# A decoder step on one core: output tiles begun inside the last pair, and the decode step's first half in sixteen pieces there

## The reference, cut to what matters

```python
# layer 0, per token t and head: state S of 64 x 64 (decode: one step on the loaded state)
sa = einsum('bhij,bhj->bhi', S, -kk_t)
S  = S * w_t[:, :, None, :] + sa[..., None] * (kk_t * a_t)[:, :, None, :] + v_t[..., None] * k_t[:, :, None, :]
y  = einsum('bhij,bhj->bhi', S, r_t)
...
out = y_gated @ w_out                       # (512 + 8) x 1024 by 1024 x 1024
...
kv  = h @ kv_w_a                            # 1024 x (256 + 64)
c_kv, k_pe = rmsnorm(kv[..., :256]), rope(kv[..., None, 256:], pos)[:, :, 0]
q   = einsum('btr,rhe->bthe', rmsnorm(q_a), w_q)   # 384 -> 8 heads x (128 + 64)
q_nope, q_pe = q[..., :128], rope(q[..., 128:], pos)
```

## Time and profile before

| | |
|---|---|
| median of three runs | 1195.48 us (1194.74 to 1195.77) |
| the profiled execution | 1196.15 us |
| its span, first to last instruction | 1194.3 us |
| mean granted TensorE clock | 0.954 |
| TensorE matmuls busy | 1074.7 us (90%) |
| VectorE busy | 512.7 us (43%) |
| ScalarE, GpSimd busy | 301.0 us, 105.7 us |

### The profile page before, as it was taken

The page is one execution under the profiler, slowest core; times in us unless marked ns, Lnnn a source line. Parts: engine busy times, 40 slices in busy tenths (PEclk is TensorE's granted clock), DMA queues, the critical chain, the costliest instruction groups (busy, mean ns, idle before and its releaser), DMA issues.

```text
span 1194.3 us, 26039 instructions
## 1 busy us (share of the span) xinstructions
PE 1074.7 (90%) x11683; PEld 767.1 (64%) x11683; DVE 512.7 (43%) x922; ACT 301.0 (25%) x565; POOL 105.7 (9%) x138
## 2 busy tenths in 40 slices
PE   2698999999999999998668887999999999999993
PEld 0466777777777767676533565887683766665563
DVE  0594455454646464555549535101120445442104
ACT  2113222223232232223011122132202344443101
POOL 0002000111111010101014120000000001000100
PEclk9799999999999999999889888999999899999897
DMA  8501021221203040402335344211211123332001
GB/s 341 210 1 71 3 89 58 75 74 59 89 10 138 2 145 2 146 2 78 139 105 223 142 195 157 88 53 64 82 71 54 71 89 125 142 131 101 1 1 71
DMA packets 18015, 110.48 MB, mean 93 GB/s; under 512 B 6888, under 2 KB 9712, under 8 KB 11760
## 3 DMA queue, kind: packets, MB, share of 16 engines
q1 hardware_dynamic: 10640, 84.57, 18.9%
q0 software_dynamic: 2304, 20.97, 4.7%
q10 hardware_dynamic: 4960, 3.27, 0.9%
HBM read 103.35 MB, written 5.19 MB: 91 GB/s over the span
## 4 chain that ended last, share of the span: by engine, by line
PE 73%; DVE 11%; issue 5%; ACT 3%; DMA 0%; ACTq 0%; DVEq 0%
PE pj L945 19%; PE pj L1378 7%; PE bk L1055 7%; PE pj L1309 5%; PE pj L1435 3%; PE pj L1305 2%; PE bk L1407 2%; PE bk L1488 2%; PE bk L878 2%; PE bk L1472 2%; PE bk L1473 1%; PE bk L1317 1%; PE bk L1010 1%; PE pj L974 1%; PE pj L1501 1%
## 5 line engine op out<-in xcount | busy, mean ns | idle before, releaser
L945 PE MATMUL pj<-XM,ring 128*128 128x260 f32 x1024 | 261.4, 396 | 0.9 <-DVE XM L1729 0.9
L945 PEld LDWEIGHTS pj<-XM,ring 128*128 128x128 f32 x1024 | 183.5, 190 | 40.6 <-issue 12.1
L1378 PE MATMUL pj<-XM,ring 128*128 128x260 f32 x352 | 80.6, 393 | 0.0
L1378 PEld LDWEIGHTS pj<-XM,ring 128*128 128x128 f32 x352 | 68.8, 196 | 11.0
L1055 PEld LDWEIGHTS bk<-arena,ring 64*64 64x64 f32 x2560 | 45.9, 137 | 35.9 <-issue 29.3
L1055 PE MATMUL bk<-arena,ring 64*64 64x64 f32 x2560 | 56.9, 228 | 8.6 <-DVE arena L1816 5.1
L878 PE MATMUL bk<-ring,cT 128*9 128x512 f32 x240 | 35.1, 685 | 21.1 <-DMA ring<-in_ada 21.1
L1822 DVE TENSOR_TENSOR arena<-arena,bk 128x512 f32<-128x512 f32 x40 | 27.5, 688 | 61.5 <-PE bk L1055 61.5
L1954 DVE TENSOR_SCALAR arena<-bk 128x512 f32<-128x512 f32 x4 | 2.8, 692 | 105.2 <-PE bk L1331 73.7
L1816 DVE TENSOR_TENSOR arena<-bk,arena 128x512 f32<-128x512 f32 x40 | 27.7, 691 | 35.0 <-PE bk L1055 34.8
L2034 DVE TENSOR_TENSOR bk<-bk,arena 128x128 f32<-128x128 f32 x32 | 9.6, 299 | 72.2 <-PE bk L1473 37.0
(11 more groups left out here) (341 smaller groups left out, 1837.6 us busy)
## 6 DMA issues: line engine op xcount, KB each, us to landing
ring<-in_ada SPq DMA_DIRECT2D x16, 2048.0 KB, 8.6
ring<-in_w_in SPq DMA_DIRECT2D x8, 2048.0 KB, 7.4
ring<-in_b_w_in SPq DMA_DIRECT2D x3, 2048.0 KB, 16.7
R<-in_xT SPq DMA_DIRECT2D x2, 2080.0 KB, 14.2
ring<-in_w_out SPq DMA_DIRECT2D x2, 2048.0 KB, 8.0
ring<-in_w_q SPq DMA_DIRECT2D x2, 1536.0 KB, 6.2
out_y<-R SPq DMA_DIRECT2D x4, 520.0 KB, 2.7
XM<-in_Sd SPq DMA_DIRECT2D x1, 2048.0 KB, 17.9
```

Source lines behind the costliest of these rows:

```text
L945: last = mm(pj[:, s, a, 0:HALF], w[:, e, k, :], XM[:, e, k, a * HALF:(a + 1) * HALF], start=(k == 0), stop=(k == KT - 1))
L1378: last = mm(pj[:, t % 2, a, 0:HALF], w[:, k, e * P:(e + 1) * P], H1[:, k, a * HALF:(a + 1) * HALF], start=(k == 0), stop=(k == KT - 1))
```

## The change

The text below numbers its parts.

1. In the last pair TensorE does `early_part(u0, u1)`: units u = 0 to 31 are one 512-column matmul each of output tiles 0 to 3 (k = u // 4, tile u % 4), 28 of them between the steps of the pair (k = 0 to 6) and four after it. `late_ada(0)` leaves the pair. To have the weights, `stream` begins with `w_out`; the late modulation groups follow in another order.
2. The six decode factors are turned in the last pair, after `chunk_products`, and stored and moved by ScalarE ahead of `operands`; plain products wait for the store (`s_dta`).
3. The product and the reduction for `sa` run as 16 pieces of 8 rows each: two in each of the levels 1 to 4 between `level_z` and `level_t`, seven in the scan, one after `center`.
4. The product of 64 x 64 for `yd` and its reduction stay behind the loop; the two products that GpSimd had go to VectorE, behind the decode result.
5. Decode rows of all 8 output tiles go through `first_rows`, in four column groups at once, behind tile 7; tiles 4 to 7 have 512 columns (`first_tile`). `out_rows(1)` in the tail uses the four groups too.
6. Key/value tiles lose the 64 swapped columns (320 instead of 384); VectorE takes the halves crosswise.
7. The queries lose their four swapped tiles (12 instead of 16). ScalarE stores the four rotary tiles, SP swaps their halves by 8 DMAs, and VectorE combines them from there. The four `qz` DMAs move behind the decode queries' latents.

The order of the ring's loads and what frees a slot:

```diff
-        stream = [("ada", LATE), ("w_out", 0), ("w_out", 1), ("ada", LATE + 1), ("ada", LATE + 2), ("ada", LATE + 3),
-                  ("b_w_in", 0), ("b_w_in", 1), ("b_w_in", 2), ("kv_w_a", 0), ("w_q", 0), ("w_q", 1), ("uk", 0)]
+        stream = [("w_out", 0), ("w_out", 1), ("ada", LATE), ("ada", LATE + 2), ("ada", LATE + 3), ("ada", LATE + 1),
+                  ("b_w_in", 0), ("b_w_in", 1), ("b_w_in", 2), ("kv_w_a", 0), ("w_q", 0), ("w_qr", 0), ("uk", 0)]
...
-            return {"w_out": (s_om, KT) if g else (s_ow, 1), "kv_w_a": (s_kvm, 5), "b_w_in": (s_bm, QT + 4 * g),
-                    "w_q": (s_bm, B_K if g else B_PE), "uk": (s_bm, B_L + 1)}[name]
+            return {"w_out": (s_ow, g + 1), "kv_w_a": (s_kvm, 5), "b_w_in": (s_bm, QT + 4 * g),
+                    "w_q": (s_bm, B_PE), "w_qr": (s_bm, B_K), "uk": (s_bm, B_L + 1)}[name]
```

SP:

```diff
-            for n in range(3, len(stream)):
+            for n in (5, 3, 4, *range(6, len(stream))):
                 sp.wait_ge(*used(n - 3))
                 load(n)
-                if n == 3:
-                    sp.wait_ge(s_dd, 4)
+                if n == 4:
+                    sp.wait_ge(s_dd, 3)
                     sp.dma_start(o["wkv_s"], Sd).then_inc(s_dso, 16)
 
+            sp.wait_ge(s_ba, B_K)
+            for b in range(4):
+                dst, src = slice(b * 32, b * 32 + 32), slice((b ^ 1) * 32, (b ^ 1) * 32 + 32)
+                sp.dma_start(qa[dst], QP[src, 0:QT, :]).then_inc(s_qsw, 16)
+                sp.dma_start(rtmp[dst], QP[src, QT, :]).then_inc(s_qsw, 16)
```

TensorE:

```diff
+            def early_part(u0, u1):
+
+                n = SI[("w_out", 0)]
+                w = ring[:, n % 3, :].rearrange("p (k e) -> p k e", k=KT)
+                for u in range(u0, u1):
+                    k, t = u // SPL, u % SPL
+                    if u == 0:
+                        arrived(n)
+                        pe.wait_ge(s_ra, 7 * PAIRS)
+                        pe.wait_ge(s_ada_out, ADA_FIRST + PAIRS - 1)
+                    if t == 0:
+                        pe.wait_ge(s_yT, k + 1)
+                    last = mm(pj[:, t // 2, t % 2, :], w[:, k, t * P:(t + 1) * P], R1[:, k, 0:T],
+                              start=(k == 0), stop=(k == KT - 1))
+                    if k == KT - 1:
+                        last.then_inc(s_om, 1)
+
+            def turn_factors():
+                pe.wait_ge(s_pp, 3 * PAIRS)
...
                 chunk_products(m, 0)
                 if more:
                     project(m + 1, 0, 4, 6)
+                else:
+                    turn_factors()
+                    early_part(0, 2)
+                    pe.wait_ge(s_dta, 1)
                 plain_products(m)
                 value_products(m)
                 turn_a(m)
                 if more:
                     project(m + 1, 0, 6, KT)
+                else:
+                    early_part(2, 4)
                 for l in range(NLEV):
                     level_z(m, l)
...
-                    elif l in (1, 2):
-                        late_ada(0, l - 1, l)
+                    else:
+                        early_part(4 + 3 * l, 6 + 3 * l)
                     level_t(m, l)
...
+                    else:
+                        early_part(6 + 3 * l, 7 + 3 * l)
                 if more:
                     project(m + 1, 3, 6, KT)
+                else:
+                    early_part(19, 20)
                 inverse_products(m)
                 if more:
                     project(m + 1, 2, 0, 2)
+                else:
+                    early_part(20, 22)
                 transition_products(m)
                 chunk_inputs(m)
                 if more:
                     project(m + 1, 2, 2, 3)
+                else:
+                    early_part(22, 23)
                 for ch in range(1, NCH):
                     scan(m, ch)
...
+                    else:
+                        early_part(20 + ch, 21 + ch)
...
+            def first_rows(g):
+
+                w = out_weights(0, g)
+                for k in range(KT):
+                    j = k % 4
+                    last = mm(bk[j * G32:j * G32 + NS, 3 - g, :], R1[:, k, T:N], w[:, k, :], start=(k < 4), stop=(k >= 4))
+                last.then_inc(s_ow, 1)
...
+            early_part(28, 32)
+            first_tile(4)
+            ada(0)
+            first_tile(5)
             ada_turn(0)
...
+            first_tile(6)
+            ada(1)
+            first_tile(7)
+            ada_turn(1)
             pe.wait_ge(s_ydm, 32)
-            tr(pj[:, 1, 1, 0:HD], ydt[0:HD, :], ident[0:HD, 0:HD]).then_inc(s_ydt, 1)
-            ada(1)
+            tr(bk[:, 2, 0:HD], ydt[0:HD, :], ident[0:HD, 0:HD]).then_inc(s_ydt, 1)
             pe.wait_ge(s_r1, 1)
...
+            first_rows(0)
+            first_rows(1)
+            turn_first_rows()
             finish_sums(0)
             ada(2)
...
-            pe.wait_ge(s_ba, B_L + 1 - 8)
+            pe.wait_ge(s_ba, B_L + 1)
             pe.wait_ge(s_qpd, 64)
             scores(0)
```

VectorE (behind the loop, the product for `yd`, its reduction and the small sums stay as they were):

```diff
+            def decode_piece(n):
+
+                step, i0 = n // 8, n % 8 * 8
+                rows = slice(i0, i0 + 8)
+                if n == 0:
+                    dve.wait_ge(s_dq, 32)
+                    dve.wait_ge(s_sd, 16)
+                    then(V.tensor_tensor(wr, dq[:, 0, :], dq[:, 5, :], ALU.mult))
+                if step % 2 == 0:
+                    x = dq[:, 3, :] if step == 0 else wr
+                    then(V.tensor_tensor(Wd1[:, rows, :], Sd[:, rows, :], x.unsqueeze(1).to_broadcast([P, 8, HD]), ALU.mult))
+                else:
+                    mark(V.tensor_reduce((sa if step == 1 else yd)[:, rows], Wd1[:, rows, :], AX_X, ALU.add))
...
             then(V.tensor_tensor(r1d, r1d, decbuf[:, 7, :, :], ALU.mult), s_r1)
-            dve.wait_ge(s_dp, 1)
+            then(V.tensor_tensor(Wd2, bj(dq[:, 2, :]), bi(1), ALU.mult))
+            mark(V.tensor_tensor(Sd, Sd, bi(5), ALU.mult))
             then(V.tensor_tensor(Wd2, Wd2, Wd1, ALU.subtract))
-            dve.wait_ge(s_dp, 2)
             then(V.tensor_tensor(Sd, Sd, Wd2, ALU.add), s_dd)
...
+            dve.wait_ge(s_qsw, 128)
             for i in range(4):
...
+                x = qa[:, i, :] if i < QT else rtmp
+                mark(V.tensor_tensor(QP[:, i, :], QP[:, i, :], cosT, ALU.mult))
+                then(V.tensor_tensor(x, x, sinT, ALU.mult))
+                then(V.tensor_tensor(QP[:, i, :], QP[:, i, :], x, ALU.add), s_bd)
```

ScalarE, behind the loop and at the `qz` DMAs:

```diff
+            for t in range(5):
+                first_tile(t)
             ada_rows(0)
...
+            first_tile(5)
             ada_tiles(0)
...
+            act.wait_ge(s_dd, 1)
             then(A(rsd, bag[:, 1:2], ACT.Ln, bias=GN_EPS))
             mark(A(rsd, rsd, ACT.Exp, scale=-0.5), s_dr)
...
+            act.wait_ge(s_dd, 2)
             for hp in range(2):
                 act.dma_start(ydt[0:HD, hp * HD:(hp + 1) * HD], yd[hp * HD:(hp + 1) * HD]).then_inc(s_ydm, 16)
...
+            first_tile(6)
...
             act.wait_ge(s_bm, base + H + 2 * TT + 1)
+            act.wait_ge(s_bd, KT + 4)
+            act.wait_ge(s_zq, 1)
+            for hp in range(2):
+                for e in range(2):
+                    act.dma_start(qz[e * ROPE:(e + 1) * ROPE, e, hp:H:2, :], QP[hp * ROPE:(hp + 1) * ROPE, :, T:N]).then_inc(s_qpd, 16)
             mark(A(qlat, bk[:, 2, 0:2 * H * NS].rearrange("p (a h s) -> p a h s", a=2, h=H), ACT.Identity), s_ba)
```

More of the change, by code:

```diff
@@ L1300, in out_tile @@
                     pe.wait_ge(s_oa, KT * layer + t - 1)
-                elif layer == 0 and t == 1:
-                    pe.wait_ge(s_lr, 1)
                 if t < SPL:
@@ L1406, in _ @@
                 for k in range(KT):
[L1407 removed]
+                    last = mm(bk[0:c, t % 2, 0:320], HK[:, k, t * P:t * P + c], kw[:, k, :],
                               start=(k == 0), stop=(k == KT - 1))
@@ L1895, in _ @@
                         prep(m + 1, "cum")
+                    if not more and l >= 1:
+                        decode_piece(2 * l - 2)
+                        decode_piece(2 * l - 1)
                     level_t(m, l)
@@ L1902, in _ @@
                         prep(m + 1, (None, "kk", None, "g", "ar", None, "bt", "rk")[ch])
+                    if not more:
+                        decode_piece(7 + ch)
                 add_outputs(m)
@@ L1907, in _ @@
                 center(m)
+                if not more:
+                    decode_piece(15)
                 if more:
@@ L2017, in _ @@
                 mark(V.tensor_tensor(kvn[0:c, t, 256:320], ps[:, 256:320], cosN[0:c, t, :], ALU.mult))
-                then(V.tensor_tensor(rt64[0:c], ps[:, 320:384], sinN[0:c, t, :], ALU.mult))
+                for e in range(2):
+                    half = slice(e * 32, e * 32 + 32)
+                    last = V.tensor_tensor(rt64[0:c, half], ps[:, 288 - 32 * e:320 - 32 * e], sinN[0:c, t, half], ALU.mult)
+                    if e == 0:
+                        mark(last)
+                then(last)
```

207 lines of the change are left out of this document (92 added, 115 removed).

## The result

The changed kernel takes 1154.57 us (median of 4 runs, 1153.01 to 1157.6) beside 1195.11 (1193.33 to 1195.77): a ratio of 0.9666 with a 95% interval from 0.9642 to 0.969. The forecast was 1160 with a range from 1150 to 1172. The profiled execution took 1155.57, its span is 1153.8; that of before had 1196.15 and 1194.3, so the profile shows 40.6 us less where the sum had 35.3.

A forecast was written before the change was run, and what follows sets the result against it. TensorE carried 73% of the chain, waiting for VectorE in the last pair and behind it. Terms of +8.7 and -19.3 (one term), -4.4, -11.2, -3.4, +8.9, -5.9 gave -35.3: 1196.15 - 35.3 - 0.67 = 1160 us, range 1150 to 1172.

The forecast's parts named there:

- terms behind the loop: From the last pair's `finish` to the norm's mean: forecast -28.0 us, with the mean itself 19.3 us earlier.
- the new wait: Layer 1, first attention scores waiting for the `qz` DMAs: +8.9 us, the upper of two bounds.
- pieces paid in full: Rival, last pair: each decode piece delays the mask or sum behind it, +11, 1171 us; chance 0.12.
- units that only lengthen the pair: Rival, last pair: output units add their own time, 24.6 instead of 8.7 us, 1176 us; chance 0.05.
- products of 11 us: Rival, behind the loop: VectorE's four products take 11.17 instead of 4.43 us each, +27, 1187 us; chance 0.04.
- The slower rival: Attention loop stays at the lower clock after 9 us of idling; 1207 us with 10 such steps; chance 0.02.
- The last pair: Last pair of the loop, filled with output units and decode pieces: longer by 8.7 us.
- Part of their time falls into waits: Last pair, two units behind the inverse products and one before the scan: only +0.9 us.
- 9 us of its gain are lost: Behind the loop: TensorE ends near 677, but VectorE's four products delay the mean to 685.7.
- The pieces at no cost: Last pair: the 16 decode pieces fit beside TensorE's work and cost nothing; uncovered, 11.0 us.
- One for one: `qz` DMAs beside GpSimd's gather: packets of both queues alternate singly, so `qz` lands at 939.1, +8.9 us.
- Decode rows: Row products in four column groups: 1.91 instead of 7.81 us, 4.1 times faster; in the tail -5.9 us.

The follow-up runs named there:

- e4: Changed kernel with all sixteen decode pieces taken out of the last pair and run behind its `finish`; median 1158.38 us, ratio 0.9684.
- e5: Changed kernel with the 28 output units taken out of the last pair and run behind it; 1173.78 us, ratio 0.9832.
- e1: Changed kernel with two of VectorE's four state products put ahead of its wait for the turned decode result; median 1156.67 us, ratio 0.9666.
- e3: Changed kernel with GpSimd's third gather of latents, 2 MB, held until the `qz` DMAs have landed; median 1155.67 us, ratio 0.9669.
- e11: Changed kernel with one matmul of 448 columns more ahead of the first scores; median 1163.63 us, ratio 0.974.
- e7: Changed kernel with two state products ahead of VectorE's wait and the `qz` DMAs issued by SP; median 1148.53 us, ratio 0.9613.
- e9: e7 with the first two output units moved later, so plain products no longer wait for `w_out`; median 1144.25 us, ratio 0.9586.

## Why the prediction was right, and where it was off

- **Right in kind and, mostly, in size.** The terms behind the loop, of the key/value tiles and of the new wait came within 1.1, 0.2 and 0.2 us. The second to fourth rivals, pieces paid in full, units that only lengthen the pair, products of 11 us, are excluded by e4, e5 and the profile. The column groups, the key/value tiles and the queries (parts 5 to 7) have no run of their own: what they gain is read from their stages. The slower rival did not occur: over the first 20 us of the loop the granted clock is 0.84, and was 0.79 before.
- **The last pair, +10.8 instead of +8.7.** Start (+2.9) and first level as forecast. Levels are 5.14, not 5.0, as TensorE never idles in them, +0.6 up to the inverse; from there to the scan's start 8.87 us against 6.70 before, where I had allowed +0.9 for three units: +2.2, with an idle of 0.80 in it. "Part of their time falls into waits" was the step that was too kind. That `finish` stands at 625.96, as forecast with 626.4, is partly luck: the pair began 2.5 earlier, with `w_out` issued and landed earlier by as much, and took 2.1 longer.
- **"9 us of its gain are lost" to VectorE.** The wait is real, its size is 5.7 by e1: TensorE's own way ends at 678.4 and not at 677, and the products end at 684.1, not at 685.7. What was not in the text is that VectorE idles 10.80 us just ahead of those four products, which is the room that e1 uses.
- **The pieces at no cost** was right, and half of the story: e4 shows that they bring nothing either, because the turned result waits for TensorE's queue. Behind the loop, where the stage to the mean is 29.1 shorter than before, e5 gives 24.7 to the units. The column groups and a VectorE without GpSimd beside it are argued for the rest; no run takes them apart.
- **The wait for `qz`, +8.9, measured +9.1.** One for one was the right end of the bounds, and the packets from 891 to 894 us show it (79 against 75). The 272 that went ahead of the gather and the 2.5 us without any were not forecast, but the last small packets come behind the gather's either way. e3 gives the two parts, 5.5 from the gather and 3.6 without it, where the lower bound had 2.6. The 9 to 17 descriptors in a turn that the Trainium skill states ("DMA: Bandwidth & Descriptors", Queues, rings and completion order) would have given an estimated +5 to +8 here; the measurement decides for the upper end.
- **Decode rows.** Four column groups were costed at 1.91 a row product, by the earlier trace rows. In the changed kernel both first products together

```profile
666.47 5.32 PE L1371 MATMUL bk<-ring,R 128*8 128x512 f32 x32 [1.69 <-DVE R L2013]
```

  take 2.66 each, at a granted 0.68; that cost nothing, as VectorE ended later. At the high clock, in e4,

```profile
669.76 3.62 PE L1371 MATMUL bk<-ring,R 128*8 128x512 f32 x32 [1.70 <-DVE R L2008]
```

  it is 1.81 each. The 7.81 of the earlier trace rows ran at a granted 0.89, so the forecast's 4.1 times compares two clocks; against 16 records of 512 columns at the high clock, 7.03, 1.81 is 3.9 times less. The estimate of 2.5 to 3.3 by the Trainium skill ("TensorE: Matmul & The Clock Gate", Part 3, Measured speedup), whose figures are for four row and three column tiles, is not borne out at that clock. In the tail it is 8.73 to 2.54 us, -6.2, at a partly low clock; but the tail gained 3.9 only, since the tile behind the row took 8.28 instead of 7.28 and the last sum 2.00 instead of 1.10, both at a lower granted clock than before (0.87 and 0.52 instead of 1.00).
- **What had no term.** The start (-2.5, of which 1.3 lie in the landing of the very first load, 13.38 against 14.68; in the eleven profiles of changed kernels the pair begins anywhere from 561.7 to 564.8), the queries and keys (another 2.0, in a stage whose clock was 0.96 and 0.91 before and 1.00 after), mean to key/value tiles (-1.5), and the attention loop with what follows (-2.6). Together -8.6; with the pair 2.1 and the tail 2.0 short of their terms, a gain of 1.1 more behind the loop, and 0.2 lost twice, that makes the 5.3 us by which the sum was too high. The attention loop, the queries and the keys ran at another granted clock than before; why, and what made the start beyond its 1.3 and the 1.5, is not shown. So the sum came out within 5.3 us with errors of both signs in it.

## What to carry to other kernels

Fill an engine's waits with work that is due later anyway, and price it by the waits: 24.6 us of TensorE's work cost 4.65 in a pair that was waiting for VectorE. Then look what each engine does while the new bound forms: here VectorE idled 10.8 us right ahead of 17.7 us of work that held up the norm, and four DMAs of 8 KB held up the scores for 9.1 us, 5.5 of them because a gather of 2 MB was issued beside them. And read small gains in their stage, since a later stretch can run at another clock for no more than one added matmul and a start moved by two us.

## What was not expected of the hardware

- The granted clock at the end of the attention loop changes with what stands 150 us ahead of it: one matmul more before the loop, which begins 1.8 us later, and the untouched 332 matmuls behind the last scores take 58.56 us at 0.90 instead of 54.77 at 0.97 (e11); the median rises by 9.7. Two profiles of one kernel agree there within 0.04 us, while timed runs of one kernel differ by up to 9 us (e1, 1149.47 to 1158.43, at mean granted clocks of 0.965 and 0.950).
- TensorE's wait for `w_out` at the start of the last pair was followed by the lower clock in two of eight profiles (e4 and e7, after 2.02 and 2.04 us of it, pairs of 66.05 and 65.73) and not in the other six (after 1.57 to 1.84 us, pairs of 61.9 to 62.5). In e9, without that wait, the pair was 61.98. That the wait decides it is not shown.
- Large operations of VectorE and GpSimd took turns here. The first two rows are of e1, where a square of GpSimd's began while one of VectorE's two early products ran, the third is GpSimd's product in the kernel before:

```profile
652.51 4.42 DVE L2007 TENSOR_TENSOR XM<-decbuf 128x4096 f32<-128x4096 f32 x1
654.04 4.01 POOL L1706 TENSOR_TENSOR R<-R 128x512 f32<-128x512 f32 x1 [6.50 <-ACT R L718]
...
623.47 7.08 POOL L1645 TENSOR_TENSOR XM<-arena 128x4096 f32<-128x4096 f32 x1 [57.87 <-DMA arena<-arena]
```

  In e1 VectorE's product took its usual 4.42. GpSimd ended 1.1 us behind it, with 4.01 instead of 1.27, and VectorE's next product, shown with e1, took 5.37 and ended 4.3 behind GpSimd. The 11.17 of the earlier trace rows reads the same way: GpSimd's product, which began 0.2 us ahead of it, ended at 630.55 and VectorE's 4.3 later, a wait of 6.9 and a product of 4.3. So the price of such a pair was here what was left of the operation that began first.
